# Second recurrence's input stage, tile by tile: three key tiles summed beside the first low-rank product

## The chip, the core and the metric

The kernel runs on one core of one Trainium2 chip. The metric is the device time of one execution in microseconds (us), the median of several runs. The engines are TensorE (PE, whose weight loads are listed apart as PEld), VectorE (DVE), ScalarE (ACT), GpSimd (POOL) and SyncE (SP, which issues the weight transfers).

## What is computed

The whole program is a two-layer hybrid network followed by a second two-layer network with a large expert lookup, in float32, for 272 tokens (256 and 16 learned ones) of width 1024. The change touches one piece of it, the inputs of the second layer's recurrence:

```python
def rwkv7_time_mix(h, mu, w_r, w_k, w_v, w0, w1, w2, a0, a1, a2, g1, g2, k_k, k_a, r_k, ln_w, ln_b, w_o):
    xx = jnp.pad(h, ((0, 0), (1, 0), (0, 0)))[:, :L] - h
    xr, xw, xk, xv, xa, xg = [h + xx * mu[i] for i in range(6)]
    r = xr @ w_r
    k = xk @ w_k
    v = xv @ w_v
    w_log = -jax.nn.softplus(-(w0 + jnp.tanh(xw @ w1) @ w2)) - 0.5
    a = jax.nn.sigmoid(a0 + (xa @ a1) @ a2)
    g = jax.nn.sigmoid(xg @ g1) @ g2
    kk = l2_normalize((k * k_k).reshape(B_, L, H, N))
    k = k * (1 + (a - 1) * k_a)
    ...
```

`h` is the normalized state. `w1` and `a1` are 1024 x 64, `g1` is 1024 x 160, the key, value and receptance weights are 1024 x 1024.

## The kernel before

The state lies with features on the 128 partitions: eight tiles (`KD` = 8) of 128 features by 272 tokens. Each engine has its own instruction list, written out by hand and run in that order; semaphores (`wait_ge`, `then_inc`) are the only order between engines. A `phase` is one block of such lists, with a barrier behind it. The function `rwkv` has the phase that this change edits, then the recurrence.

In that phase DVE finishes the norm (`norm_dve`, L244), writes eight tiles of `xn` (L1595), the difference to the previous token `xx` in two instructions over all tiles (L1598, L1599), and then blends `xn + mu * xx` with eight instructions per input (`blend`, L1553): first the one for the decay product, into `mix_a`, then the one for the rate product, into `mix_b`. Semaphores `mixed_w`, `mixed_a`, `mixed_k`, `mixed_g` count the finished tiles of each.

PE runs, in this order: the decay input product `w1` and the rate input product `a1` (both L1503, eight matmuls each with 64 output columns); their two output products (L1510, 8 + 8 matmuls, each waiting for a free bank among four "side" banks, 4 to 7); the eight key tiles (`project`, L1486, banks 0 to 3 in turn); the two gate input products (L1519); eight pairs of gate output products (L1524, L1525), which first wait for ACT's two gate sigmoids; the value tiles with the head sums (L1486, L1534); the receptance tiles. Every float32 matmul appears in the trace as two passes, so "x16" is eight matmuls.

ACT takes the side banks: Tanh and Copy (L1647) into `hw`, sixteen sigmoids (L1651) into `cum` and `a_`. Then for each key tile `m` it waits for `cum_ready` and, from `m` = 2, for DVE's key tile `m` - 2 (`grown_read`), and runs three exponentials (L1656 to L1658). Behind the last come `decay_mid` and `decay_end` (L1659, L1660) and only then the gate sigmoids (L1664).

DVE, when the decay values are there, sums them up in two halves (`sum_decay`, L1562 to L1567), blends the gate input, and takes each key tile with six instructions (`take_key`, L1574 to L1581), the first three of which read the bank and the last three of which need ACT's exponentials.

SP loads the key weights: the first four tiles in the phase before, the others when the first tiles are done (`k_ready`).

Of the kernel before, what the change touches and what calls it, by code (L numbers as in the profile page):

```python
# [12 lines left out]
ALU = mybir.AluOpType  # L13
# [278 lines left out]
def first_block(nc, a, w, x, xn, norm, late_const, cst, vcs, psum, psum_all):  # L292
# [1151 lines left out]
    def rwkv(g, kept, lora):  # L1444
# [3 lines left out]
        with ExitStack() as cx:  # L1448
# [3 lines left out]
            with ExitStack() as c0:  # L1452
                cum = sb("rw_cum", [P, KD, TP], c0)
                xx = sb("xx", [P, KD, T], c0)
                mix_a, mix_b = sb("mix_a", [P, KD, T], c0), sb("mix_b", [P, KD, T], c0)
                hw = bonus[0:64, 0:2, :]
                temp = norm.squares
                hg = temp[:, 0, :], temp[0:32, 1, :]
# [3 lines left out]
                with phase(nc, *NORM, "mixed_w", "mixed_a", "mixed_k", "mixed_g", "mixed_v", "mixed_r", "side", "side_read", "k_ready", "k_free",  # L1462
# [9 lines left out]
                    def _(pe):  # L1472
# [27 lines left out]
                        for n, (wt, src, mixed) in enumerate(((lora.w1, mix_a, S.mixed_w), (lora.a1, mix_b, S.mixed_a))):  # L1500
                            for q in range(KD):
                                pe.wait_ge(mixed, q + 1)
                                mm = pe.matmul(side_bank(n)[0:64, :], wt[:, q, :], src[:, q, :], start=(q == 0), stop=(q == KD - 1))  # L1503
                            mm.then_inc(S.side, 1)
# [6 lines left out]
                        for m in range(KD):  # L1511
                            if m >= 4:
                                pe.wait_ge(S.k_free, m - 3)
                            project(0, m, mix_a, S.mixed_k, S.k_ready)
                        for n, (m0, mn) in enumerate(((0, P), (P, 32))):
# [4 lines left out]
                            mm.then_inc(S.side, 1)  # L1520
                        pe.wait_ge(S.side_read, GATE_OUT)
# [24 lines left out]
                    def _(dve):  # L1546
# [23 lines left out]
                        def take_key(m):  # L1570
# [5 lines left out]
                            dve.scalar_tensor_tensor(out=k[:, m, 0:T], in0=temp[:, m % 2, :], scalar=1.0, in1=banks[m % 4], op0=ALU.add, op1=ALU.mult).then_inc(S.k_free, 1)  # L1576
                            dve.wait_ge(S.exps, m + 1)
# [16 lines left out]
                        for m in range(KD):  # L1594
                            last = dve.scalar_tensor_tensor(out=xn[:, m, :], in0=x[:, m, :], scalar=gain[:, m:m + 1], in1=norm.rs[:, :],  # L1595
                                                            op0=ALU.mult, op1=ALU.mult)
                        step(last)
                        dve.tensor_scalar(xx[:, :, 0:1], xn[:, :, 0:1], -1.0, None, ALU.mult)  # L1598
                        step(dve.tensor_tensor(xx[:, :, 1:T], xn[:, :, 0:T - 1], xn[:, :, 1:T], ALU.subtract))  # L1599
                        blend(MU_W, mix_a, S.mixed_w)  # L1600
                        blend(MU_A, mix_b, S.mixed_a)
# [4 lines left out]
                        blend(MU_K, mix_a, S.mixed_k)  # L1606
                        sum_decay(slice(0, 4))
                        sum_decay(slice(4, 8))
                        dve.wait_ge(S.side, 2)
                        blend(MU_G, mix_b, S.mixed_g)  # L1610
                        dve.wait_ge(S.k_ready, 1)
                        step(dve.memset(k[:, :, T:TP], 0.0))
                        for m in range(KD):
                            take_key(m)
                        dve.wait_ge(S.k_ready, KD)
# [26 lines left out]
                    def _(act):  # L1642
# [18 lines left out]
                        act.wait_ge(S.k_free, KD)  # L1661
# [7 lines left out]
                        def square_key(m):  # L1669

                            if m >= 2:
                                act.wait_ge(S.side, KK_SUM + m - 1)
                            act.wait_ge(S.kk_raw, m + 1)
                            act.activation(temp[:, m % 2, :], kk[:, m, 0:T], ACT.Square).then_inc(S.kk_squares, 1)

                        square_key(0)
# [1611 lines left out]
```

## Time and profile before

| What | Value |
|---|---|
| Median of 3 runs | 3508.43 us (3508.38 to 3513.5) |
| The profiled execution's own time | 3508.08 us |
| Its span in the trace | 3506.3 us |
| Mean granted TensorE clock | 0.957 of full |
| PE busy | 91% of the span |
| DVE busy | 63% of the span |
| ACT busy | 20% of the span |

The span is what the profiler records of the core; 1.8 us of that execution lie around it. The phase of the change runs from about 963 to 1109 us of the span. In rows of the timeline, the first number is the start, the second the time to the end of the last of the merged instructions, and the bracket the idle time ahead of them and who ended it. Clock 1.00 is 2.4 GHz, 0.50 is 1.2 GHz.

### The profile page before, as it was taken

The numbers are of one execution on the slowest core, as the hardware profiler recorded it, in microseconds if no ns is written. First come the engines' busy times: TensorE is split into PE (matmuls) and PEld (weight loads), VectorE is DVE, ScalarE is ACT, GpSimd is POOL, SyncE is SP. The second block draws the span as 40 slices with busy tenths as digits, with TensorE's granted clock in tenths as the row PEclk, the third lists the DMA queues.
The fourth block names the chain that finished last, engine by engine and source line by source line (L and its number), as shares of the span: only waits on it lengthen the run. The fifth ranks groups of instructions, "written<-read, shape, count | busy, mean of one in ns | idle before, by whom it ended". The sixth has DMA issues, their size and how long they took to land. (4 is left out here: it accounts for less than half of the span.)

```text
span 3506.3 us, 54158 instructions
## 1 busy us (share of the span) xinstructions
PE 3179.8 (91%) x20154; PEld 2378.5 (68%) x20154; DVE 2199.1 (63%) x5583; ACT 710.7 (20%) x1749; POOL 595.9 (17%) x516
## 2 busy tenths in 40 slices
PE   8999889999989999999998978887899988888887
PEld 8997479999968979987885433343578864344433
DVE  7843648778676548732447777776414468677775
ACT  1110321111131211101322222222212322222222
POOL 0000000000000000000004544444100035444442
PEclk9999599999999999999998999999999999999988
DMA  5443014454412014452349999999634479999997
GB/s 188 161 167 121 1 61 157 161 180 173 141 58 88 4 73 169 161 203 84 120 192 389 421 421 422 422 421 422 274 128 157 168 289 421 421 422 422 422 422 329
DMA packets 116002, 829.00 MB, mean 236 GB/s; under 512 B 12784, under 2 KB 14320, under 8 KB 17424
## 3 DMA queue, kind: packets, MB, share of 16 engines
q0 software_dynamic: 73728, 536.90, 36.8%
q1 hardware_dynamic: 39488, 273.59, 21.4%
q10 hardware_dynamic: 2576, 15.59, 1.3%
q8 instruction: 146, 2.39, 0.3%
q14 instruction: 64, 0.52, 0.0%
HBM read 824.99 MB, written 1.05 MB: 236 GB/s over the span
## 5 line engine op out<-in xcount | busy, mean ns | idle before, releaser
L3013 PE MATMUL psum_all<-expert_rows,const_sb 128*128 128x512 f32 x2048 | 963.7, 628 | 186.1 <-ACT const_sb L2925 185.0
L2612 POOL DMA_INDIRECT expert_rows<-in_peer_uv_dram,head_experts x512 | 595.7, 1164 | 2865.6 <-issue 1944.4
L3013 PEld LDWEIGHTS psum_all<-expert_rows,const_sb 128*128 128x128 f32 x2048 | 401.4, 200 | 730.7 <-issue 468.7
L2764 DVE CUSTOM_DVE_ANT_0 expert_rows<-expert_rows,xn 128x1024 f32<-128x1024 f32 x512 | 616.7, 1223 | 263.2 <-DMA expert_rows<-in_peer_uv_dram,head_experts 259.2
L2268 PE MATMUL psum_all<-x,weight_ring 128*128 128x256 f32 x1024 | 228.6, 381 | 0.0
L2925 ACT ACTIVATE const_sb<-cst,head_weights 128x128 f32<-128x128 f32 x496 | 158.6, 390 | 324.4 <-DVE head_weights L2775 299.9
L2268 PEld LDWEIGHTS psum_all<-x,weight_ring 128*128 128x128 f32 x1024 | 191.7, 190 | 28.8 <-issue 3.5
L407 PE MATMUL psum_all<-xn,weight_ring 128*128 128x136 f32 (+1 forms) x1408 | 193.5, 281 | 15.4 <-PEq L174 9.5
L407 PEld LDWEIGHTS psum_all<-xn,weight_ring 128*128 128x128 f32 x1408 | 177.9, 193 | 16.2 <-DMA weight_ring<-in_ffn_in_dram 9.5
L280 PE MATMUL psum_all<-xn,weight_ring 128*128 128x272 f32 (+1 forms) x640 | 147.7, 394 | 2.5 <-DVE expert_rows L2211 1.4
L407 PE MATMUL psum_all<-xn,weight_sums 128*128 128x136 f32 (+1 forms) x1056 | 143.5, 279 | 0.6 <-DVEq L631 0.6
L280 PEld LDWEIGHTS psum_all<-xn,weight_ring 128*128 128x128 f32 x640 | 123.4, 193 | 26.4 <-DVE expert_rows L2211 2.2
L2921 ACT ACTIVATE dots<-dots 128x4 f32<-128x4 f32 x124 | 25.4, 205 | 560.5 <-DVE dots L2764 560.5
L407 PE MATMUL psum_all<-input_sums,weight_sums 128*128 128x136 f32 (+1 forms) x1056 | 133.2, 279 | 0.1
L407 PEld LDWEIGHTS psum_all<-xn,weight_sums 128*128 128x128 f32 x1056 | 131.8, 192 | 1.0 <-issue 1.0
L407 PEld LDWEIGHTS psum_all<-input_sums,weight_sums 128*128 128x128 f32 x1056 | 127.2, 192 | 0.4 <-issue 0.4
L516 ACT ACTIVATE gate<-gate 128x272 f32<-128x272 f32 (+1 forms) x88 | 37.5, 427 | 359.4 <-DVE gate L601 359.4
L561 DVE TENSOR_TENSOR weight_sums<-weight_ring 128x512 f32<-128x512 f32 (+1 forms) x102 | 68.4, 671 | 59.1 <-PE psum_all L407 55.7
L407 PE MATMUL psum_all<-hidden,weight_ring 128*128 128x136 f32 (+1 forms) x704 | 88.6, 278 | 0.0
L2995 PE MATMUL psum_all<-x,weight_ring 128*128 128x256 f32 x384 | 84.8, 379 | 0.0
L407 PEld LDWEIGHTS psum_all<-hidden,weight_ring 128*128 128x128 f32 x704 | 84.5, 190 | 0.0
L2995 PEld LDWEIGHTS psum_all<-x,weight_ring 128*128 128x128 f32 x384 | 73.0, 190 | 15.0 <-issue 5.7
(579 smaller groups left out, 4806.8 us busy)
## 6 DMA issues: line engine op xcount, KB each, us to landing
weight_ring<-in_ffn_in_dram SPq DMA_DIRECT2D x88, 1024.0 KB, 4.9
weight_ring<-in_w_in_dram SPq DMA_DIRECT2D x48, 1024.0 KB, 4.8
weight_ring<-in_ffn_out_dram SPq DMA_DIRECT2D x32, 1024.0 KB, 5.1
weight_ring<-in_ffn_out_dram SPq DMA_DIRECT2D x16, 768.0 KB, 4.3
weight_ring<-in_hyb_in_dram SPq DMA_DIRECT2D x12, 1024.0 KB, 4.9
weight_ring<-in_peer_q_dram SPq DMA_DIRECT2D x12, 1024.0 KB
expert_rows<-in_w_v_dram ACTq DMA_DIRECT2D x8, 1024.0 KB
weight_ring<-in_br_attn_dram SPq DMA_DIRECT2D x8, 1024.0 KB, 7.2
```

Source lines behind the costliest of these rows:

```text
L280: mm = pe.matmul(banks[s * halves + h], wt[:, h, k, :], rhs[:, k, :], start=(k == 0), stop=(k == ktiles - 1))
L407: mm = pe.matmul(out, left(j), right(j), start=first and j == js[0], stop=end and j == js[-1], skip_group_check=onto)
L516: act.activation(gate[:, p % 2, :], gate[:, p % 2, :], ACT.Silu).then_inc(S.gate_ready, 1)
L561: dve.tensor_tensor(ws[:, 0], wt[:, 1, :, 0, :], wt[:, 1, :, 1, :], ALU.add).then_inc(S.weight_sums, 1)
L2268: mm = pe.matmul(late_bank(t)[:, half * T2:(half + 1) * T2], wt[:, half, k, :], h[:, k, :], start=(k == 0), stop=(k == KD - 1))
L2612: pool.indirect_dma_start(out=rows[:, j, :], out_offset=None, in_=a["peer_uv"], in_offset=bass.IndirectOffsetOnAxis(ap=idx[:, n, j:j + 1], ...
L2764: dve.tensor_tensor_reduce(row, row, xt[:, n, :], 1.0, 0.0, ALU.mult, ALU.add, dots[:, n, j:j + 1]).then_inc(S.dotted, 1)
L2921: act.activation(dots[:, n, at], dots[:, n, at], ACT.Gelu_apprx_tanh).then_inc(S.gelus, 1)
L2925: act.activation(diag[:, j, :], ident, ACT.Copy, scale=wts[:, n, j:j + 1]).then_inc(S.diagonals, 1)
L2995: mm = pe.matmul(query_bank[:, c, :], wt[:, c, k, :], h[:, k, :], start=(k == 0), stop=(k == KD - 1))
L3013: mm = pe.matmul(sums(n, half), diag[:, j, :], rows[:, j, D + half * 512:D + (half + 1) * 512], start=False, stop=last and j == TOPK - 1)
```

## The change

It adds a third buffer `mix_c`, rewrites DVE's first steps tile by tile, and reorders all three engines' lists. `take_key` is cut in two: what reads the bank stays, what needs the exponentials becomes `grow_key`.

```diff
-                mix_a, mix_b = sb("mix_a", [P, KD, T], c0), sb("mix_b", [P, KD, T], c0)
+                mix_a, mix_b, mix_c = (sb(name, [P, KD, T], c0) for name in ("mix_a", "mix_b", "mix_c"))
-                hg = temp[:, 0, :], temp[0:32, 1, :]
+                hg = mix_c[:, 0, :], mix_c[0:32, 1, :]
...
# PE
-                        for n, (wt, src, mixed) in enumerate(((lora.w1, mix_a, S.mixed_w), (lora.a1, mix_b, S.mixed_a))):
-                            for q in range(KD):
-                                pe.wait_ge(mixed, q + 1)
-                                mm = pe.matmul(side_bank(n)[0:64, :], wt[:, q, :], src[:, q, :], start=(q == 0), stop=(q == KD - 1))
-                            mm.then_inc(S.side, 1)
+                        early_tiles = []
+                        for s in range(2):
+                            pe.wait_ge(w.landed[g % 2][s], 16)
+                            wt = w.slot(g % 2, s, W2).rearrange("p (h k m) -> p h k m", h=2, k=KD)
+                            early_tiles += [wt[:, 0], wt[:, 1]]
+                        for q in range(KD):
+                            pe.wait_ge(S.mixed_k, q + 1)
+                            for m in range(3):
+                                mm = pe.matmul(banks[m], early_tiles[m][:, q, :], mix_a[:, q, :], start=(q == 0), stop=(q == KD - 1))
+                                if q == KD - 1:
+                                    mm.then_inc(S.k_ready, 1)
+                            pe.wait_ge(S.mixed_w, q + 1)
+                            mm = pe.matmul(side_bank(0)[0:64, :], lora.w1[:, q, :], mix_b[:, q, :], start=(q == 0), stop=(q == KD - 1))
+                        mm.then_inc(S.side, 1)
+                        project(0, 3, mix_a, S.mixed_k, S.k_ready)
+                        for q in range(KD):
+                            pe.wait_ge(S.mixed_a, q + 1)
+                            mm = pe.matmul(side_bank(1)[0:64, :], lora.a1[:, q, :], mix_c[:, q, :], start=(q == 0), stop=(q == KD - 1))
+                        mm.then_inc(S.side, 1)
...
-                        for m in range(KD):
-                            if m >= 4:
-                                pe.wait_ge(S.k_free, m - 3)
-                            project(0, m, mix_a, S.mixed_k, S.k_ready)
...
+                        for m in range(4, KD):
+                            pe.wait_ge(S.k_free, m - 3)
+                            project(0, m, mix_a, S.mixed_k, S.k_ready)
...
# DVE
+                        for m in range(KD + 2):
+                            if m < KD:
+                                dve.scalar_tensor_tensor(out=xn[:, m, :], in0=x[:, m, :], scalar=gain[:, m:m + 1], in1=norm.rs[:, :],
+                                                         op0=ALU.mult, op1=ALU.mult).then_inc(S.xn_ready, 1)
+                            if 1 <= m <= KD:
+                                q = m - 1
+                                dve.wait_ge(S.xn_ready, q + 1)
+                                dve.tensor_scalar(xx[:, q, 0:1], xn[:, q, 0:1], -1.0, None, ALU.mult)
+                                dve.tensor_tensor(xx[:, q, 1:T], xn[:, q, 0:T - 1], xn[:, q, 1:T], ALU.subtract).then_inc(S.xx_ready, 1)
+                            if m >= 2:
+                                q = m - 2
+                                dve.wait_ge(S.xx_ready, q + 1)
+                                for mu, dst, mixed in ((mu_k, mix_a, S.mixed_k), (mu_w, mix_b, S.mixed_w)):
+                                    dve.scalar_tensor_tensor(out=dst[:, q, :], in0=xx[:, q, :], scalar=mu[:, q:q + 1], in1=xn[:, q, :],
+                                                             op0=ALU.mult, op1=ALU.add).then_inc(mixed, 1)
+                        blend(MU_A, mix_c, S.mixed_a)
...
                         dve.wait_ge(S.side, 1)
-                        blend(MU_K, mix_a, S.mixed_k)
+                        blend(MU_G, mix_b, S.mixed_g)
                         sum_decay(slice(0, 4))
+                        dve.wait_ge(S.side, GATE_IN)
+                        step(dve.memset(k[:, :, T:TP], 0.0))
+                        for m in range(4):
+                            take_key(m)
+                        grow_key(0)
+                        grow_key(1)
                         sum_decay(slice(4, 8))
-                        dve.wait_ge(S.side, 2)
-                        blend(MU_G, mix_b, S.mixed_g)
-                        dve.wait_ge(S.k_ready, 1)
-                        step(dve.memset(k[:, :, T:TP], 0.0))
-                        for m in range(KD):
+                        grow_key(2)
+                        grow_key(3)
+                        for m in range(4, KD):
                             take_key(m)
+                            grow_key(m)
...
# ACT
-                        act.wait_ge(S.k_free, KD)
                         for n in range(2):
                             act.wait_ge(S.side, GATE_IN + n + 1)
                             act.activation(hg[n], side_bank(GATE_IN + n)[0:hg[n].shape[0], :], ACT.Sigmoid).then_inc(S.side_read, 1)
...
+                        act.wait_ge(S.k_free, KD)
                         square_key(0)
```

On PE, from the end of the norm to the gate output products, the list before reads (`rw_v` holds `w1`, `rw_k` holds `a1` and `w2a2`, `rw_gate` holds `g1`, `weight_ring` the key weights; here "x8" counts matmuls, not passes):

```order
L231 MATMUL psum_all<-norm_sums,cst 128x272
L232 MATMUL psum_all<-norm_squares,cst 128x272
L1503 MATMUL psum_all<-mix_a,rw_v 64x272 x8
L1503 MATMUL psum_all<-mix_b,rw_k 64x272 x8
L1510 MATMUL psum_all<-rw_bonus,rw_k 128x272 x16
L1486 MATMUL psum_all<-mix_a,weight_ring 128x272 x64
L1519 MATMUL psum_all<-mix_b,rw_gate 128x272 x8
L1519 MATMUL psum_all<-mix_b,rw_gate 32x272 x8
L1524 MATMUL psum_all<-norm_squares,rw_v 128x272
```

With the change, the same place from the last of eight rounds (each an L1508 row and an L1512 row) on:

```order
L1508 MATMUL psum_all<-mix_a,weight_ring 128x272 x3
L1512 MATMUL psum_all<-mix_b,rw_v 64x272
L1486 MATMUL psum_all<-mix_a,weight_ring 128x272 x8
L1517 MATMUL psum_all<-mix_c,rw_k 64x272 x8
L1524 MATMUL psum_all<-rw_bonus,rw_k 128x272 x16
L1529 MATMUL psum_all<-mix_b,rw_gate 128x272 x8
L1529 MATMUL psum_all<-mix_b,rw_gate 32x272 x8
L1486 MATMUL psum_all<-mix_a,weight_ring 128x272 x32
L1537 MATMUL psum_all<-mix_c,rw_v 128x272
```

Three and then one key tile moved ahead of the rate product, the gate inputs moved ahead of the other four, and the decay product is spread over the first rounds: the number of output columns goes from 128 to 64 and back in each round.

On DVE, at the start of the phase, the list before reads:

```order
L244 RECIPROCAL norm_rs<-norm_rs 128x272
L1595 SCALAR_TENSOR_TENSOR xn<-x,vcs,norm_rs 128x272 x8
L1598 TENSOR_SCALAR xx<-xn 128x8
L1599 TENSOR_TENSOR xx<-xn 128x8x271
L1553 SCALAR_TENSOR_TENSOR mix_a<-xx,vcs,xn 128x272 x8
L1553 SCALAR_TENSOR_TENSOR mix_b<-xx,vcs,xn 128x272 x8
```

and with the change, up to the second tile's first instruction after the first two blends:

```order
L244 RECIPROCAL norm_rs<-norm_rs 128x272
L1613 SCALAR_TENSOR_TENSOR xn<-x,vcs,norm_rs 128x272 x2
L1618 TENSOR_SCALAR xx<-xn 128x1
L1619 TENSOR_TENSOR xx<-xn 128x271
L1613 SCALAR_TENSOR_TENSOR xn<-x,vcs,norm_rs 128x272
L1618 TENSOR_SCALAR xx<-xn 128x1
L1619 TENSOR_TENSOR xx<-xn 128x271
L1624 SCALAR_TENSOR_TENSOR mix_a<-xx,vcs,xn 128x272
L1624 SCALAR_TENSOR_TENSOR mix_b<-xx,vcs,xn 128x272
```

The first blend, which PE waits for, stood behind ten instructions of all tiles and now stands behind seven of single tiles.

Further down DVE's list, between the first half's decay sums and the fifth key tile, the changed order is this (L1597 is the last instruction of `grow_key(1)`; L1575 to L1580 are the second half's `sum_decay`; L1587 is the first of `take_key(4)`):

```order
L1597 TENSOR_TENSOR rw_k<-rw_k,norm_rs 128x272
L1575 SCALAR_TENSOR_TENSOR rw_kk_r<-early_cst,rw_cum 128x320 x4
L1577 COPY rw_decay_mid<-rw_kk_r 128x20
L1578 TENSOR_TENSOR rw_kk_r<-rw_kk_r,rw_decay_mid 128x1280
L1579 COPY rw_decay_end<-rw_kk_r 128x20
L1580 TENSOR_TENSOR rw_cum<-rw_kk_r,rw_cum 128x1280
L1594 TENSOR_TENSOR rw_a<-rw_a,norm_sums 128x272
L1596 TENSOR_SCALAR rw_bonus<-rw_k,vcs 128x272
L1597 TENSOR_TENSOR rw_k<-rw_k,norm_sums 128x272
```

Before, both `sum_decay` halves stood ahead of the first key tile; now the second half stands behind four `take_key` and two `grow_key`, and six key tiles' `grow_key` stand behind it. ACT's order is unchanged but for the wait on `k_free`.

## Rows read from the trace of the kernel before

**Rows 1.** The page's head

```profile
span 3506.3 us, 54158 instructions
```

**Rows 2.** Busy by stretch: length, PE, PEld, DVE, ACT, POOL, granted clock, DMA

```profile
974.21:1029.94 55.73, 55.00 (x224) 40.19 (x224) 48.26 (x109) 21.82 (x49) 0.00 (x0) 0.95 0.20 76
```

**Rows 3.** Timeline, from the key weights' load to the second low-rank product

```profile
942.64 0.80 SPq L196 DMA_DIRECT2D weight_ring<-in_rwkv_k_dram  x2
...
967.61 3.39 DVE L1595 SCALAR_TENSOR_TENSOR xn<-x,vcs,norm_rs 128x272 f32<-128x272 f32 x8
...
971.12 2.40 DVE L1599 TENSOR_TENSOR xx<-xn 128x2168 f32<-128x2168 f32 x1
973.56 3.39 DVE L1553 SCALAR_TENSOR_TENSOR mix_a<-xx,vcs,xn 128x272 f32<-128x272 f32 x8
...
974.21 6.56 PE L1503 MATMUL psum_all<-mix_a,rw_v 128*64 128x272 f32 x16 [8.95 <-DVE mix_a L1553]
...
980.61 3.83 PE L1503 MATMUL psum_all<-mix_b,rw_k 128*64 128x272 f32 x16
```

**Rows 4.** Stretches with their granted clock (columns as in rows 2)

```profile
974.21:979.75 5.54, 5.54 (x13) 2.86 (x14) 5.54 (x14) 0.00 (x0) 0.00 (x0) 0.50 0.01 3
...
1109.21:1112.75 3.54, 3.54 (x37) 3.54 (x39) 0.19 (x1) 0.00 (x0) 0.00 (x0) 0.53 0.01 2
...
1107.14:1109.21 2.07, 0.00 (x1) 0.03 (x1) 1.40 (x3) 0.00 (x0) 0.00 (x0) 1.00 0.00 0
...
516.00:524.00 8.00, 5.47 (x32) 4.44 (x31) 3.98 (x8) 1.62 (x5) 0.00 (x0) 1.00 0.26 79
```

**Rows 5.** Timeline, output products, sigmoids and decay sums

```profile
984.37 2.10 PE L1510 MATMUL psum_all<-rw_bonus,rw_k 64*128 64x272 f32 x8
984.48 0.39 ACT L1647 ACTIVATE rw_bonus<-psum_all 64x272 f32<-64x272 f32 x1 [3.28 <-PE psum_all L1503]
...
986.18 3.16 ACT L1651 ACTIVATE rw_cum<-psum_all,vcs 128x272 f32<-128x272 f32 x8
986.70 2.97 DVE L1562 TENSOR_TENSOR_SCAN rw_kk_r<-early_cst,rw_cum 128x320 f32<-128x320 f32 x4 [1.80 <-ACT rw_cum L1651]
...
993.17 2.97 DVE L1562 TENSOR_TENSOR_SCAN rw_kk_r<-early_cst,rw_cum 128x320 f32<-128x320 f32 x4
```

**Rows 6.** Timeline, key tiles on PE, DVE and ACT

```profile
992.42 29.60 PE L1486 MATMUL psum_all<-mix_a,weight_ring 128*128 128x272 f32 x128
...
1003.07 0.38 DVE L1612 MEMSET rw_k<- 128x384 f32 x1
1003.49 0.50 DVE L1574 TENSOR_SCALAR rw_kk_r<-psum_all,vcs 128x272 f32<-128x272 f32 x1
...
1004.64 0.43 DVE L1578 TENSOR_TENSOR rw_a<-rw_a,norm_sums 128x272 f32<-128x272 f32 x1
...
1005.74 0.50 DVE L1574 TENSOR_SCALAR rw_kk_r<-psum_all,vcs 128x272 f32<-128x272 f32 x1
1005.92 0.43 ACT L1656 ACTIVATE norm_sums<-rw_kk_r 128x272 f32<-128x272 f32 x1 [9.28 <-DVE rw_k L1581]
...
1017.19 0.43 ACT L1656 ACTIVATE norm_rs<-rw_kk_r 128x272 f32<-128x272 f32 x1 [1.04 <-DVE rw_k L1581]
...
1018.30 0.22 ACT L1659 ACTIVATE rw_decay_mid<-rw_decay_mid 128x40 f32<-128x40 f32 x1
```

**Rows 7.** Timeline, gate inputs, gate sigmoids, first gate outputs

```profile
1021.86 7.61 PE L1519 MATMUL psum_all<-mix_b,rw_gate 128*128 128x272 f32 x32
...
1025.61 3.35 PEld L1519 LDWEIGHTS psum_all<-mix_b,rw_gate 128*32 128x32 f32 x16 [0.36 <-issue]
1025.77 1.28 ACT L1664 ACT_TABLE_LOAD   x1 [7.12 <-PE psum_all L1519]
...
1029.94 0.73 PE L1524 MATMUL psum_all<-norm_squares,rw_v 128*128 128x272 f32 x2 [0.48 <-ACT norm_squares L1664]
...
1030.60 0.72 PE L1525 MATMUL psum_all<-norm_squares,rw_v 32*128 32x272 f32 x2
```

More of the change, by code:

```diff
@@ L1461, in rwkv @@
                 side_bank = lambda n: banks[4 + n % 4]
-                with phase(nc, *NORM, "mixed_w", "mixed_a", "mixed_k", "mixed_g", "mixed_v", "mixed_r", "side", "side_read", "k_ready", "k_free",
+                with phase(nc, *NORM, "xn_ready", "xx_ready", "mixed_w", "mixed_a", "mixed_k", "mixed_g", "mixed_v", "mixed_r", "side", "side_read", "k_ready", "k_free",
                            "v_ready", "v_free", "r_ready", "r_free", "cum_ready", "exps", "grown_read", "kk_raw", "kk_squares", "kk_root", "kk_done",
@@ L1576, in take_key, with grow_key @@
                             dve.scalar_tensor_tensor(out=k[:, m, 0:T], in0=temp[:, m % 2, :], scalar=1.0, in1=banks[m % 4], op0=ALU.add, op1=ALU.mult).then_inc(S.k_free, 1)
+                        def grow_key(m):
                             dve.wait_ge(S.exps, m + 1)
@@ L1593, in _ @@
                         gain = vec(vcs, "mix_norm", KD, KD)
-                        for m in range(KD):
[L1595 to L1601, printed above, removed]
+                        mu_k, mu_w = vec(vcs, "mu", MU_K * KD, KD), vec(vcs, "mu", MU_W * KD, KD)
+                        for m in range(KD + 2):
[14 more added lines that the diff above has]
+                        blend(MU_A, mix_c, S.mixed_a)
                         for t in (a_, kk, cum):
@@ L1605, in _ @@
                         dve.wait_ge(S.side, 1)
-                        blend(MU_K, mix_a, S.mixed_k)
+                        blend(MU_G, mix_b, S.mixed_g)
                         sum_decay(slice(0, 4))
-                        sum_decay(slice(4, 8))
-                        dve.wait_ge(S.side, 2)
-                        blend(MU_G, mix_b, S.mixed_g)
-                        dve.wait_ge(S.k_ready, 1)
-                        step(dve.memset(k[:, :, T:TP], 0.0))
-                        for m in range(KD):
+                        dve.wait_ge(S.side, GATE_IN)
[4 more added lines that the diff above has]
+                        grow_key(1)
+                        sum_decay(slice(4, 8))
+                        grow_key(2)
+                        grow_key(3)
+                        for m in range(4, KD):
                             take_key(m)
+                            grow_key(m)
                         dve.wait_ge(S.k_ready, KD)
```

## The prediction, written before the changed kernel ran

> **What bounds the kernel now.** I read the head of the page first: the span is 3506.3 us [rows 1], and the profiled execution took 3508.08 us, 0.35 us under the median of 3508.43. The sum below is in the trace's time; what it saves or costs is taken off or put on the median. Next I read the stretches. From PE's first product of this phase to its first gate output product it is busy 55.00 of 55.73 us [rows 2], so in that stretch the phase is as long as PE's list, and a change can gain only by starting PE earlier, by cheaper PE work, or by removing the 0.73 us of waits. The timeline then shows what precedes the stretch: PE idles 8.95 us until the first blend of `mix_a` exists, while DVE does eight `xn` tiles (from 967.61), the two `xx` instructions (from 971.12), and starts blending at 973.56; PE starts at 974.21 [rows 3]. That head is what the change attacks. All else in the phase, from the gate outputs at 1029.94 on, is untouched in order, so I only have to ask: **when does the first gate output start now?** Its start at 1029.94 [rows 7] is my yardstick.
>
> **PE's earlier start.** A blend or `xn` tile costs 3.39/8 = 0.42 us [rows 3]. The `xx` instruction takes 2.40 us for 8 x 271 elements; a tile of it is then 0.30 plus a fixed part, and with the one-column instruction I take 0.44 per tile. Ahead of the first blend stand three `xn` and two `xx` tiles: 3 x 0.42 + 2 x 0.44 = 2.15, so it starts at 967.61 + 2.15 = 969.76 instead of 973.56, and with the same 0.65 us from there to PE, PE starts at 970.41: **3.80 us earlier**. From then on DVE needs 0.42 + 0.44 + 2 x 0.42 = 1.71 us per tile. A round on PE is eight passes, 8 x 0.229 = 1.84 us at clock 1.00 (a pass is (992.42 to 1021.86)/128 = 0.230 or, from the rate product, 3.67/16 = 0.229 [rows 3, 6, 7]) and 3.6 at 0.50, so PE is the slower and DVE stays ahead of it; as the first rounds run at 0.50, DVE would have to need over 2.2 us per tile to hold it up. The key weights were asked for at 942.64, 28 us ahead of PE's new start, so they are no new wait [rows 3].
>
> **The clock at the start.** PE ran at 0.50 for its first 5.54 us of work [rows 4], and the decay product took 6.40 us instead of 3.67. I take the same 5.54 us again. The nearest other restart kept 0.50 for 3.54 us [rows 4]; that would save half the difference, 1.0 us.
>
> **The rounds.** 64 passes: 5.54 us at 0.453 (6.40 us held 12 such and 4 fast ones) is 12 passes, the other 52 take 11.93, together 17.47 us. New is the change of shape, 128 to 64 columns and back, 16 times. No row has exactly that. Bounds: from the 128-column to the 32-column gate input, where the weight load starts 0.36 us late, 32 passes of 0.229 and the 0.16 us by which a row outlasts its passes (3.83 against 3.67) would end at 1021.86 + 7.34 + 0.16 = 1029.36, and the row ends at 1029.47 [rows 3, 7]: 0.1 per change. The gate outputs change from 128 to 32 rows at each matmul: 1029.94 to 1030.60 is 0.66 us for two passes instead of 0.46, so 0.2 per change [rows 7]. The lower end is 0: the loads may be hidden under the other passes. A column change is nearest to the first row, so I take 0.1: 1.6 us (ends: 0 and 3.2). The Trainium skill, "TensorE: Matmul & The Clock Gate", Part 2, step LDWEIGHTS, says that weight loads are pulled ahead of running matmuls where row groups don't conflict, or into the background buffer. By that the rounds would cost nothing extra; the gate output row, with its 0.2, shows that it is not so for every mix of shapes, and no row here shows it for this one.
>
> **From there to the gate outputs.** Rounds end at 970.41 + 17.47 + 1.6 = 989.5. Key tile 3 takes 3.67 (993.2), the rate product 3.67 and about 0.2 for its two shape changes (997.0). In the kernel before that point was 984.37 [rows 5]: the rate product, and with it ACT's and DVE's chain, is now **12.6 us later**, while PE's remaining work is shorter. So two chains meet at the gate outputs:
> - PE: output products 984.37 to 992.42 = 8.05, gate inputs 7.6, four key tiles 4 x 3.68 = 14.7: 30.4 us [rows 5 to 7], ready at 1027.4.
> - DVE and ACT. ACT releases the gate outputs behind the exponentials of key tile 7, which wait for `grow_key(5)`. From the start of the output products to the end of the first decay half: 993.17 - 984.37 = 8.80 [rows 5]. Memset 0.42. Four `take_key` of 1004.64 - 1003.49 = 1.15: 4.60. Two `grow_key` of 1005.74 - 1004.64 = 1.10: 2.20. Second decay half 993.17 - 986.70 = 6.47. Two `grow_key` 2.20, then keys 4 and 5 complete, 2 x 2.25 = 4.50 [rows 5, 6]. DVE sum: 29.19. Then ACT: 0.18 to start, 1017.19 to 1018.30 = 1.11 for the three exponentials, 0.35 for the two small ones, 1.29 table load, two sigmoids 0.7, 0.04 to PE: 3.67 [rows 6, 7]. Together **32.86 us**, ready at 1029.9.
>
> So the gate outputs start at 1029.9 against 1029.94. The head start of 3.8 us, and the wait of 0.48 that goes, are paid away: 1.8 us to changes of shape and 2.5 us to a new stall, PE waiting from 1027.4 to 1029.9 for the gate sigmoids, because DVE's decay sums now start late. Gain: **about 0.1 us**. DVE is done with key 7 some 3 us behind the old time, but the value blend (3.4 us) is needed only 10.5 us after the gate outputs begin, so nothing further is late.
>
> **A rule on the table load.** The switch from copy to sigmoid on ACT goes from 984.48 + 0.39 to 986.18: 1.3 us in all [rows 5], and that is what stands in my sum. The Trainium skill, "ScalarE: Activation LUTs", What ACT_TABLE_LOAD costs, puts a switch at about 2.66 us, since a drain of 1.38 comes with it. By that the new stall would be 1.4 us longer and the kernel 1.3 us slower. The row speaks against it.
>
> **The rivals.**
> 1. *Shape changes are free.* All chains shift by 1.8: gate outputs at 1028.1, gain 1.9, 3506.5 us. For: another weight load can hide; against: rows 7.
> 2. *They cost 0.2 each.* 1.6 us later: 3509.9.
> 3. *The new stall lowers the clock.* Ahead of the recurrence PE idled 2.07 us and then ran 3.54 us at 0.50; inside 516 to 524 it idled 2.5 us and the clock stayed at 1.00 [rows 4]. So it can go either way. Price: 3.5 us at half rate, less what the gate outputs' shape gaps hide, 1.4 us: 3509.7. By the table-load rule the time would be about the same, 3509.7, by another cause.
> 4. *Slower, on one mechanism: the tile-by-tile rounds keep PE at 0.50.* If PE paused in each round for DVE, the clock might not rise until the rounds end. 52 passes at 0.453 instead of 0.229 are 11.6 us: 3519.9. It decides once over 31 passes more (7.1/0.224) run at 0.50. Against: DVE needs 1.71 us per tile, PE at 0.50 3.6, so no pause is left to it.
> 5. *DVE and ACT are not behind.* If the decay sums overlapped more than I think and the stall vanished, gate outputs start at 1027.4: gain 2.5, with free shapes 4.3, 3504.1. That is the most that this change can give; it is under 7 us.
>
> **How the numbers follow.** About 7 us, 0.2%, is what a measurement of this kernel can tell from no change. Chances: forecast (3508.3, own range 3507 to 3509.5) 0.35; rival 1 0.20; rival 2 0.12; rival 3 0.17 with the table-load rule's 0.03 in it; rival 4 0.02; rival 5 0.10; scatter or a shift elsewhere that leaves these cases 0.04. The costs' bounds give 3504.1 to about 3511.3 (rivals 2 and 3 together), and the shown runs spread by 5.1 us upward, so the range is 3504 to 3512.5. Only rival 4 and part of the scatter lie beyond 0.2% on the slow side, 0.03; on the fast side only scatter, 0.03; the rest, 0.94, is the same.
>
> **What the profile of the changed kernel would show.** PE's first L1508 pass 2.8 to 2.9 us behind the end of the norm's reciprocal; the L1512 passes on a grid of 1.84 us (free shapes) or 2.0 (0.1 each) at clock 1.00; rate product's end 12 to 13 us later than 984.37; a single wait of 2 to 3 us of PE ahead of L1537 with ACT's gate sigmoid as its releaser; the first L1537 within 2 us of 1029.9; the same durations from there on. The prediction would be wrong if PE waited inside the rounds for DVE, if the stall ahead of L1537 were over 4 us or absent, or if the clock stood at 0.50 beyond some 6 us.

## The result, and the profile after

The changed kernel takes 3515.05 us in the median of 20 executions (3507.85 to 3524.64), the kernel before 3507.77 us (3503.59 to 3513.85, 20 executions): a ratio of 1.0022 with a 95% interval of 1.0014 to 1.003. It is 7.3 us slower, outside my range of 3504 to 3512.5. The times fall into two kinds: ten of the 20 lie at 3507.9 to 3513.4 us, ten at 3516.7 to 3524.6 us. The median of 3515.05 lies between them, where no execution is: the middle of the first kind is 3511.8 us, 4.0 over the kernel before, that of the second 3521.4. The traced execution took 3508.97 us, so it is one of the first kind.

From the page of that execution, the head and PE's busy time; the span answers to [rows 1]:

```profile
span 3507.2 us, 54172 instructions
...
PE 3184.6 (91%) x20154; PEld 2378.6 (68%) x20154; DVE 2200.6 (63%) x5597; ACT 711.1 (20%) x1749; POOL 599.4 (17%) x516
```

The timeline of the phase's start, which answers to [rows 3], with one round of the later ones:

```profile
967.47 1.85 DVE L244 RECIPROCAL norm_rs<-norm_rs 128x272 f32<-128x272 f32 x1 [3.45 <-ACT norm_rs L238]
...
971.43 0.50 DVE L1624 SCALAR_TENSOR_TENSOR mix_a<-xx,vcs,xn 128x272 f32<-128x272 f32 x1
...
972.07 3.06 PE L1508 MATMUL psum_all<-mix_a,weight_ring 128*128 128x272 f32 x6 [5.06 <-DVE mix_a L1624]
...
975.06 1.17 PE L1512 MATMUL psum_all<-mix_b,rw_v 128*64 128x272 f32 x2
...
982.87 0.67 PE L1512 MATMUL psum_all<-mix_b,rw_v 128*64 128x272 f32 x2
...
983.48 1.64 PE L1508 MATMUL psum_all<-mix_a,weight_ring 128*128 128x272 f32 x6
985.05 0.67 PE L1512 MATMUL psum_all<-mix_b,rw_v 128*64 128x272 f32 x2
...
992.18 3.93 PE L1486 MATMUL psum_all<-mix_a,weight_ring 128*128 128x272 f32 x16
```

The trace starts 1.74 us later at this point than that of before, from stages that no edit touches, so I count from the start of the reciprocal. In the kernel before these rows, with the value tile behind the gate outputs, read:

```profile
965.73 1.85 DVE L244 RECIPROCAL norm_rs<-norm_rs 128x272 f32<-128x272 f32 x1 [3.45 <-ACT norm_rs L238]
...
1040.40 3.93 PE L1486 MATMUL psum_all<-mix_a,weight_ring 128*128 128x272 f32 x16
1044.17 0.62 PE L1534 MATMUL psum_all<-norm_squares,early_cst 128*128 128x272 f32 x2
```

PE starts after 4.60 us instead of 8.48: 3.88 us earlier. It never waits for DVE in the rounds, but a round takes 985.05 - 982.87 = 2.18 us (2.17 in the mean of five), against eight passes of 0.229 = 1.83.

The timeline from the output products to the value tiles answers to [rows 5 to 7]:

```profile
999.85 2.10 PE L1524 MATMUL psum_all<-rw_bonus,rw_k 64*128 64x272 f32 x8
...
1007.90 7.72 PE L1529 MATMUL psum_all<-mix_b,rw_gate 128*128 128x272 f32 x32
...
1015.54 14.93 PE L1486 MATMUL psum_all<-mix_a,weight_ring 128*128 128x272 f32 x64
...
1023.76 0.43 ACT L1686 ACTIVATE norm_sums<-rw_kk_r 128x272 f32<-128x272 f32 x1 [6.36 <-DVE rw_k L1597]
...
1030.84 1.28 ACT L1693 ACT_TABLE_LOAD   x1
...
1032.13 0.66 ACT L1693 ACTIVATE mix_c<-psum_all 128x272 f32<-128x272 f32 x2
...
1032.85 0.73 PE L1537 MATMUL psum_all<-mix_c,rw_v 128*128 128x272 f32 x2 [2.37 <-ACT mix_c L1693]
1033.51 0.72 PE L1538 MATMUL psum_all<-mix_c,rw_v 32*128 32x272 f32 x2
1034.16 0.72 PE L1537 MATMUL psum_all<-mix_c,rw_v 128*128 128x272 f32 x2
...
1043.30 3.93 PE L1486 MATMUL psum_all<-mix_a,weight_ring 128*128 128x272 f32 x16
```

PE waits 2.37 us for the gate sigmoids, as forecast, and the gate outputs begin 65.38 us after the reciprocal's start instead of 64.21. They take 1043.30 - 1032.85 = 10.45 us, the same as before (1029.94 to 1040.40). In this execution the gate outputs and all behind them come 1.2 us later, and nothing in it explains a median 7 us up. For that a trace of the second kind was needed.

### The profile page after: what moved, and what is told of

Its sections match the earlier page's. It is cut to its first block and busy times, and to the rows that moved or that the text cites. A ratio compares the mean times of both kernels' runs of the same rounds, so it can differ in the third digit from the quotient of the medians.

```text
span 3507.2 us, 54172 instructions
## 1 busy us (share of the span) xinstructions
PE 3184.6 (91%) x20154; PEld 2378.6 (68%) x20154; DVE 2200.6 (63%) x5597; ACT 711.1 (20%) x1749; POOL 599.4 (17%) x516
```

## The experiments

Three theories stood against each other for the second kind of execution. **A**: the rounds, with their changes of shape, hold PE at 0.50 for much longer. **B**: the new wait ahead of the gate outputs lets the clock fall, and the gate outputs then keep it at 0.50. **C**: the time is lost elsewhere. "Phase" below is the time from the start of the reciprocal to the first head-sum product of the value tiles, 78.44 us in the kernel before (1044.17 - 965.73; 78.53 in a second trace of it) and 79.60 in the first trace of the changed one. Every set of runs has executions of the kernel before beside it on the same chip, and the ratios are to those; their medians are 3508.33 us for `again1`, `four1`, `gate1` and `both1`, 3508.97 for `stall`, `dense`, `late` and `group`, and 3508.32 for `short`, `again_b`, `group_a` and `before_a`.

### The changed kernel again

Label `again1`, no edit.

> The changed kernel once more, unedited, for its spread and a second trace. All theories: a median 3 to 13 us over the kernel before, and times from about 3508 to 3525 us. If the trace falls on a slow execution it tells at once where the time is: theory A (the rounds of three key tiles and one decay product keep PE at 0.50 for much longer than 5.9 us) has the rounds at some 30 us instead of 20.1; theory B (PE's wait of 2.4 us ahead of the gate outputs lowers the clock) has the rounds at 20 us and the gate outputs at 14 to 17 us instead of 10.5; theory C (the time is lost elsewhere, in the expert stage or by where the code lies) has neither.

All five executions took 3517.37 to 3522.51 us, median 3520.01 (ratio 1.0036, 1.0023 to 1.005), and the trace, with a span of 3515.8 us, is one of the second kind. Its timeline of PE at the gate outputs:

```profile
1021.80 3.83 PE L1486 MATMUL psum_all<-mix_a,weight_ring 128*128 128x272 f32 x16
1027.99 1.28 PE L1537 MATMUL psum_all<-mix_c,rw_v 128*128 128x272 f32 x2 [2.36 <-ACT mix_c L1693]
1029.19 1.27 PE L1538 MATMUL psum_all<-mix_c,rw_v 32*128 32x272 f32 x2
1030.39 1.28 PE L1537 MATMUL psum_all<-mix_c,rw_v 128*128 128x272 f32 x2
...
1046.04 1.27 PE L1538 MATMUL psum_all<-mix_c,rw_v 32*128 32x272 f32 x2
1047.24 6.08 PE L1486 MATMUL psum_all<-mix_a,weight_ring 128*128 128x272 f32 x16
1053.16 0.62 PE L1547 MATMUL psum_all<-norm_squares,early_cst 128*128 128x272 f32 x2
```

and its stretches (length, busy of PE, PEld, DVE, ACT, POOL, granted clock, DMA):

```profile
1026.00:1028.50 2.50, 0.51 (x1) 0.50 (x2) 2.40 (x8) 1.92 (x3) 0.00 (x0) 0.85 0.01 3
1028.50:1050.00 21.50, 21.50 (x38) 9.67 (x37) 7.02 (x17) 3.50 (x9) 0.00 (x0) 0.50 0.00 1
1050.00:1054.00 4.00, 4.00 (x15) 3.14 (x15) 0.00 (x0) 0.58 (x2) 0.00 (x0) 0.80 0.00 0
```

The wait is the same 2.36 us, but behind it every two passes take 1.20 us instead of 0.66, at clock 0.50, to the end of the gate outputs and through most of the first value tile. Gate outputs: 1047.24 - 1027.99 = 19.25 us instead of 10.45; value tile 1053.16 - 1047.24 = 5.92 instead of 3.77. Together 10.95 us. The phase is 90.7 us; the rounds are as in the first trace, with the clock back at 1.00 some 6 us after PE's start. The clock had fallen at 1027.73, 2.1 us into the wait, and was back at 1051.62. This is theory B's picture and not A's. Outside the phase the two traces of this kernel differ too, by 5.0 us less ahead of the reciprocal and 2.5 us more behind the phase, so of the 11.1 us in the phase 8.6 are left in the span. Note that the profile shows PE 100% busy all through those 21.5 us.

A third set of the unedited kernel, `again_b`:

> The changed kernel a third time, on the same chip as the others of this call. Half or more of the executions at 3516 us and over, the rest at 3508 to 3513. In its trace the gate outputs take either 10.5 us at clock 1.00 or 17 to 19 us, mostly at 0.50; nothing between and no other place that differs by more than 3 us.

Six executions, median 3521.01 us (ratio 1.0035, 1.0023 to 1.0047): 3510.26 and 3512.17, and four from 3520.90 to 3524.36, with nothing between. The traced one is the 3510.26: the phase is 79.6 us, the wait 2.37 us, no fall. That no other place would differ by over 3 us failed: the reciprocal starts at 965.7 us here, at 962.5 in `again1`, at 967.5 in the first trace. Over the two sets 9 of 11 executions are of the second kind, in the first measurement 10 of 20.

### Rounds of one shape

Label `four1`.

```diff
-                            for m in range(3):
+                            for m in range(4):
                                 mm = pe.matmul(banks[m], early_tiles[m][:, q, :], mix_a[:, q, :], start=(q == 0), stop=(q == KD - 1))
...
+                        for q in range(KD):
                             pe.wait_ge(S.mixed_w, q + 1)
                             mm = pe.matmul(side_bank(0)[0:64, :], lora.w1[:, q, :], mix_b[:, q, :], start=(q == 0), stop=(q == KD - 1))
                         mm.then_inc(S.side, 1)
-                        project(0, 3, mix_a, S.mixed_k, S.k_ready)
```

> All four early key tiles in the rounds, so that a round is eight passes of one shape, and the decay product behind them in one piece; everything else as in the changed kernel. In the trace every theory expects a round at 1.84 us instead of 2.17, the rounds with the decay product and key tile 3 some 2.5 us shorter, the gate outputs 2.5 us earlier, the wait ahead of them still 2.4 us. Theory A expects the executions around 3520 to be gone: all times at 3504 to 3510 us, at or 1 to 2 us under the kernel before. Theory B expects them to stay, in about half of the executions, as the wait is still there: from 3505 up to 3522. Theory C expects both kinds too.

Median 3517.43 us over eight executions (3510.74 to 3518.82), ratio 1.0023 (1.0013 to 1.0034). Five of the eight are above 3516 us: the second kind stays, so theory A is out. In its trace PE waits 1028.00 to 1030.35, the clock falls at 1032.6, 2.3 us after the gate outputs began, and is back at 1.00 at 1053.1; its stretches, in the columns of `again1`:

```profile
1028.00:1032.60 4.60, 2.25 (x7) 1.18 (x8) 4.50 (x13) 2.68 (x7) 0.00 (x0) 1.00 0.01 2
1032.60:1053.10 20.50, 20.50 (x38) 10.14 (x38) 5.29 (x13) 3.10 (x8) 0.00 (x0) 0.50 0.00 1
```

The gate outputs start 2.6 us earlier than in the first trace, as expected, and the phase is 86.5 us. Gate outputs and first value tile take 23.8 us against 14.2 in the kernel before: the fall costs 9.5 us here.

### Gate sigmoids earlier

Label `gate1`.

```diff
                         for m in range(KD):
+                            if m == 4:
+                                for n in range(2):
+                                    act.wait_ge(S.side, GATE_IN + n + 1)
+                                    act.activation(hg[n], side_bank(GATE_IN + n)[0:hg[n].shape[0], :], ACT.Sigmoid).then_inc(S.side_read, 1)
                             act.wait_ge(S.cum_ready, m // 4 + 1)
...
-                        for n in range(2):
-                            act.wait_ge(S.side, GATE_IN + n + 1)
-                            act.activation(hg[n], side_bank(GATE_IN + n)[0:hg[n].shape[0], :], ACT.Sigmoid).then_inc(S.side_read, 1)
```

> The gate sigmoids of ScalarE moved ahead of the exponentials of key tile 4, where ScalarE otherwise waits 6 us for the second half of the decay sums; one more table load there, everything else as in the changed kernel. In the trace every theory expects PE's wait of 2.4 us ahead of the gate outputs to go, and the gate outputs 2.4 us earlier. Theory B expects the executions around 3520 to be gone: all times at 3504 to 3511 us. Theory A expects them to stay, each 2.4 us less: about 3506 to 3522. Theory C expects both kinds too.

Median 3509.67 us over 11 executions (3506.71 to 3515.69), ratio 1.0008 (0.9999 to 1.0017). No execution is at 3516 or above, where theory A and C wanted about half. Against the 3520.01 of `again1`, on the same chip, removing one wait of 2.4 us took 10 us off the median, and the wait alone can't do that. Theory B's upper end was missed: five of the 11 lie above 3511. In the trace the wait is gone, the clock stays at 1.00 from 976.8 to the end of the phase, and the phase is 77.2 us; that is the second fastest of the 11 executions, so it doesn't show what the slower ones do.

### Both

Label `both1`, the two edits together.

> Both edits together: rounds of one shape and early gate sigmoids. Gate outputs some 4 to 5 us earlier than in the changed kernel, counted from the end of the norm. Theories A and B both expect only the fast kind of execution, 3502 to 3508 us, some 3 to 4 us under the kernel before. Theory C still expects about half of the executions 10 us longer.

Median 3507.9 us over 11 executions (3502.46 to 3510.99), ratio 0.9998 (0.9989 to 1.0007). The local part came as expected; from the timeline:

```profile
969.56 17.89 PE L1508 MATMUL psum_all<-mix_a,weight_ring 128*128 128x272 f32 x64 [5.07 <-DVE mix_a L1624]
987.39 3.88 PE L1513 MATMUL psum_all<-mix_b,rw_v 128*64 128x272 f32 x16
...
1010.56 14.93 PE L1486 MATMUL psum_all<-mix_a,weight_ring 128*128 128x272 f32 x64
...
1012.42 1.28 ACT L1686 ACT_TABLE_LOAD   x1
1013.72 0.67 ACT L1686 ACTIVATE mix_c<-psum_all 128x272 f32<-128x272 f32 x2
...
1018.75 1.28 ACT L1690 ACT_TABLE_LOAD   x1 [4.37 <-DVE rw_k L1597]
...
1025.33 0.62 PE L1537 MATMUL psum_all<-mix_c,rw_v 128*128 128x272 f32 x2
1025.88 0.72 PE L1538 MATMUL psum_all<-mix_c,rw_v 32*128 32x272 f32 x2
```

The first 64 passes take 987.39 - 969.56 = 17.83 us with one shape, against 992.18 - 972.07 = 20.11 with two; PE goes from the keys to the gate outputs without a wait. The phase is 74.49 us, 4.0 less than before, yet the median is only 0.4 us under that of before, where 3 to 4 were expected, and five of the 11 lie above 3508. The traced execution is the fastest. More on this below.

### The wait alone, in the kernel before

The direct test of theory B: labels `stall` and `short` repeat the second gate sigmoid in the kernel before, each time waiting for its own end.

```diff
                         for n in range(2):
                             act.wait_ge(S.side, GATE_IN + n + 1)
+                            for _ in range(5 if n else 0):
+                                step(act.activation(hg[n], side_bank(GATE_IN + n)[0:hg[n].shape[0], :], ACT.Sigmoid))
```

> The kernel before, with the second gate sigmoid repeated five times, so that PE waits some 2.5 to 2.8 us ahead of the gate outputs instead of 0.48; nothing else changed. If a wait there costs only itself, all executions are 2.2 us longer, about 3510.5. Theory B (the wait lowers the clock, and the gate outputs that follow keep it at 0.50 until the value tiles) expects in addition some 10 us in half or more of the executions: times from 3508 to 3524, a median of 3515 to 3520. Theory A (the rounds) has no rounds here and expects 3510.5.

Median 3518.7 us over nine executions (3514.85 to 3520.4), ratio 1.0027 (1.0017 to 1.0037). A wait of 2.56 us in the place of 0.48 costs the kernel before 9.7 us, and not one of the nine is at the 3510.5 us of a wait that costs only itself. Its trace shows where, on PE's timeline:

```profile
1032.46 0.72 PE L1524 MATMUL psum_all<-norm_squares,rw_v 128*128 128x272 f32 x2 [2.56 <-ACT norm_squares L1666]
1033.12 0.72 PE L1525 MATMUL psum_all<-norm_squares,rw_v 32*128 32x272 f32 x2
...
1034.42 0.92 PE L1525 MATMUL psum_all<-norm_squares,rw_v 32*128 32x272 f32 x2
1035.27 1.27 PE L1524 MATMUL psum_all<-norm_squares,rw_v 128*128 128x272 f32 x2
1036.47 1.27 PE L1525 MATMUL psum_all<-norm_squares,rw_v 32*128 32x272 f32 x2
```

The first pair and a half run at full rate, then the clock falls, 2.4 us after PE has resumed, and stays at 0.50 for 20.5 us, until 1055.3. The phase is 90.15 us, 11.7 more than before: 2.1 are the longer wait and 9.5 the fall. With `range(2 if n else 0)`:

> The kernel before with the second gate sigmoid repeated twice instead of five times: PE waits about 1.4 us ahead of the gate outputs (0.48 before, 2.6 in the run with five). If a wait there costs in proportion, all times are 0.9 us longer, about 3510. If it works through the fall of the clock, the share of executions that fall shrinks with the wait: median 3510 to 3514 us, with a few times at 3518 and over.

Median 3512.48 us over 11 executions (3506.86 to 3515.95), ratio 1.0011 (1.0002 to 1.002). No execution reached 3516, and the traced one, with a wait of 1.31 us, has no fall; the phase is 79.4 us. But that is the fastest of the 11, so it doesn't show whether slower ones had a short fall. The few times at 3518 and over that were expected did not come. The median is 4.2 us up where the wait explains 0.8; where the other 3 us go in these executions is not shown.

### Gate outputs in groups

Label `dense`: the changed kernel with its wait, but denser gate outputs.

```diff
-                        for m in range(KD):
-                            side_free(GATE_OUT + m)
-                            pe.matmul(side_bank(GATE_OUT + m), lora.g2[:, m * P:(m + 1) * P], hg[0], start=True, stop=False)
-                            pe.matmul(side_bank(GATE_OUT + m), lora.g2b[:, m * P:(m + 1) * P], hg[1], start=False, stop=True).then_inc(S.side, 1)
+                        for first in (0, 4):
+                            for m in range(first, first + 4):
+                                side_free(GATE_OUT + m)
+                                pe.matmul(side_bank(GATE_OUT + m), lora.g2[:, m * P:(m + 1) * P], hg[0], start=True, stop=False)
+                            for m in range(first, first + 4):
+                                pe.matmul(side_bank(GATE_OUT + m), lora.g2b[:, m * P:(m + 1) * P], hg[1], start=False, stop=True).then_inc(S.side, 1)
```

> The changed kernel with the wait of 2.4 us kept, but the gate outputs in two groups of four: four 128-row matmuls, then four 32-row ones, so that the shape changes 4 times instead of 16. In a trace at clock 1.00 the gate outputs take 8.0 us instead of 10.5. If it is the pauses between shapes that keep the clock at 0.50 once it has fallen, a fall lasts 3 to 7 us here instead of 20 and costs 2 to 3 us: all times at 3505 to 3513 us. If the wait alone decides, and the pauses don't matter, slow executions stay at 3516 or more.

Median 3512.63 us over 11 executions (3509.64 to 3518.02), ratio 1.0012 (1.0003 to 1.0021): one execution above 3516, and five above the 3513 that were the expected end. The trace caught a fall, and shows how short it is:

```profile
1033.30 3.62 PE L1538 MATMUL psum_all<-mix_c,rw_v 128*128 128x272 f32 x8 [2.36 <-ACT mix_c L1695]
1036.85 2.10 PE L1540 MATMUL psum_all<-mix_c,rw_v 32*128 32x272 f32 x8
1038.88 2.10 PE L1538 MATMUL psum_all<-mix_c,rw_v 128*128 128x272 f32 x8
...
1042.93 3.94 PE L1486 MATMUL psum_all<-mix_a,weight_ring 128*128 128x272 f32 x16
```

The clock fell at 1033.0 and was back at 1.00 at 1036.4, 3.1 us after PE resumed. All eight pairs took 9.63 us in spite of it, and the phase is 78.9 us. In `again1` the clock fell at the same point of the same wait (2.1 us into it in both), so the two differ by the order of the gate outputs: 3.4 us at 0.50 here, 23.9 there. The alternation of shapes is what holds the clock down; that it works by the pauses at each change is the likely reason, not shown apart. It is one trace of a short fall, but the times bear it out: one of 11 executions above 3516, against 19 of 31 of the changed kernel. The median is still 3.7 us over the kernel before, of which the phase explains 0.4.

### The head start alone, undone

Label `late`: as `both1`, with VectorE's start as in the kernel before.

```diff
-                        for m in range(KD + 2):
...
+                        for m in range(KD):
+                            last = dve.scalar_tensor_tensor(out=xn[:, m, :], in0=x[:, m, :], scalar=gain[:, m:m + 1], in1=norm.rs[:, :],
+                                                            op0=ALU.mult, op1=ALU.mult)
+                        step(last)
+                        dve.tensor_scalar(xx[:, :, 0:1], xn[:, :, 0:1], -1.0, None, ALU.mult)
+                        step(dve.tensor_tensor(xx[:, :, 1:T], xn[:, :, 0:T - 1], xn[:, :, 1:T], ALU.subtract))
+                        blend(MU_K, mix_a, S.mixed_k)
+                        blend(MU_W, mix_b, S.mixed_w)
```

> As the kernel with one shape in the rounds and early gate sigmoids, but VectorE's old start: all xn tiles, both xx instructions over all tiles, then the key blend and the decay blend in one piece each. What the tile-by-tile start is worth by itself: PE's first product 3.4 to 3.8 us later, counted from the end of the norm, and the gate outputs as much later; 3.5 us slower than the kernel with both edits, 3509 to 3513 us.

Median 3509.82 us over 11 executions (3507.8 to 3515.3), ratio 1.0007 (0.9998 to 1.0016). PE's first product comes 8.49 us after the reciprocal's start against 4.60, 3.9 us later (3.8 in the prediction), but the phase is 78.04 us against 74.49: 3.55 us. PE's first work runs at 0.50 for 5.4 us here and for 6.0 in `both1`, and that takes back 0.3. In the medians, each set against its own runs of the kernel before, `late` is 0.9 us over and `both1` 0.4 under: the start is worth 1.3 us there, where 3.5 were expected.

### All three, and the kernel before again

Label `group`: both edits and the grouped gate outputs.

> Both edits (rounds of one shape, early gate sigmoids) and the gate outputs in groups of four. No wait over 0.5 us ahead of the gate outputs, and these 2.4 us shorter: in a trace the value tiles start 7 us earlier than in the kernel before, counted from the end of the norm. Theory B expects only fast executions, 3500 to 3508 us, a median some 4 us under the kernel before.

Median 3508.44 us over 11 executions, ratio 0.9995 (0.9986 to 1.0004). The gate outputs on PE's timeline:

```profile
1028.46 2.00 PE L1538 MATMUL psum_all<-mix_c,rw_v 128*128 128x272 f32 x8
1030.39 2.10 PE L1540 MATMUL psum_all<-mix_c,rw_v 32*128 32x272 f32 x8
1032.41 2.10 PE L1538 MATMUL psum_all<-mix_c,rw_v 128*128 128x272 f32 x8
1034.44 2.10 PE L1540 MATMUL psum_all<-mix_c,rw_v 32*128 32x272 f32 x8
1036.47 3.93 PE L1486 MATMUL psum_all<-mix_a,weight_ring 128*128 128x272 f32 x16
```

They take 8.01 us instead of 10.45, and the phase 72.1, 6.4 us less than before. The median is 0.5 us under the kernel before, where some 4 were expected. Once more, with a second trace (`group_a`), and the kernel before itself (`before_a`):

> The kernel with both edits and grouped gate outputs once more, for its time and a second trace. The phase at 72.0 us as in its first trace. If the 5 us that its first trace lost between the recurrence's end and the next network were chance, that stage is at 353 us now and the median comes to 3503 to 3505 us; if they belong to the kernel, it is at 357 again and the median at 3508.

> The kernel before once more, for a second trace of it: how far do stages that no edit touches differ between two executions of one kernel. Median at 3508 to 3509 us; the phase of the change at 78.5 us from the norm's reciprocal to the first head sum of the value tiles; the stage from the recurrence's end to the next network's first layer at 352 to 354 us, the rest within 3 us of the first trace.

`group_a`: median 3506.83 us over 11 executions (3503.37 to 3508.83), ratio 0.9994 (0.9985 to 1.0003). `before_a`: 3508.14 us, ratio 1.0001 (0.9992 to 1.001). The stage from the recurrence's end (the first product of its last norm) to the next network's first layer takes 357.4 and 357.1 us in the two traces of `group`, 352.6 and 353.0 in those of the kernel before. So 4.4 of the 6.4 us are given back there, both times: of the two cases that I had written down, chance is out. It isn't `group`'s code alone either: the trace of `short`, where nothing of that stage and nothing of DVE's order was edited, has 356.5. Around the recurrence's output norm the clock falls twice in every trace: for 6.8 us each in the kernel before, for 10.2 us each in `group`, for 6.8 and 10.2 in `short`. Other stages differ between two traces of one kernel: one ahead of the phase takes 185.7 and 182.2 us in the kernel before, over the 3 us that I expected as the most.

## Why the prediction was wrong

Point by point, by its own steps:

- **PE's earlier start**: 3.80 forecast, 3.88 measured. Right. DVE needs 1.65 us per tile (1.71 forecast), and PE never waits for it in the rounds.
- **The clock at the start**: 5.54 forecast, 5.7 us measured at 0.50 (972.07 to 977.80). Right.
- **The rounds**: 17.47 + 1.6 = 19.07 us forecast, 20.11 measured. The term of the shape changes was mis-sized: a round is 0.34 us longer than eight passes, 0.17 per change, where I took 0.1 within ends of 0 and 0.2. With the slightly longer low stretch that is 1.0 of the 1.2 us by which the first trace's gate outputs miss; the rest is in the chain below.
- **From there to the gate outputs**: DVE's and ACT's chain 32.86 us forecast, 1032.85 - 999.85 = 33.00 measured; the new wait 2.5 forecast, 2.37 measured. Right, to a tenth or two.
- **The table load**: 1030.84 to 1032.13, 1.29 us, and no drain behind it. By the Trainium skill's rule ("ScalarE: Activation LUTs", What ACT_TABLE_LOAD costs) it would be 2.66; this trace disagrees and the measurement decides.
- **The step that failed is the price of rival 3, "the new stall lowers the clock"**: "3.5 us at half rate, less what the gate outputs' shape gaps hide, 1.4 us". The sum itself, 3508.3 us, had this cost at nothing. The runs show 10.95 us in `again1` and 9.5 in `four1` and `stall`. It is what takes the median out of the range: the first kind's middle, 3511.8 us, is inside, the second's, 3521.4, is not. It is also the one of my signs of being wrong that came true, the clock at 0.50 beyond some 6 us. I took the length of the low stretch from dense work behind another gap [rows 4], and put it onto gate outputs that alternate between 128 and 32 rows. `again1`, `four1` and `stall` show that such work did not bring the clock back: it stayed at 0.50 for 20 to 24 us, into the first value tile. `dense` shows the cause: the same wait with grouped shapes has 3.4 us at 0.50, and its gate outputs are 1.6 us longer than the 8.01 of `group`, close to my 1.4. And I had counted the shape gaps as a relief, as time that the low clock doesn't lengthen; two passes took 1.20 us instead of 0.66, the gap lengthened with them.
- **The chance of that rival**, 0.17, was also low: 19 of 31 executions of the changed kernel are of the second kind. The rows I had seen (a fall behind a gap of 2.07 us, none behind one of 2.5 us) are two of eleven gaps of PE over 2 us in the first 1600 us of that trace. At two, of 2.52 and 2.43 us, the clock stayed at 1.00; one, of 8.95, lies in a low stretch already begun; at the other eight, of 2.07 to 5.71 us, it fell, in the gap or up to 2.4 us behind it. All of them had to be read before a new one of 2.5 could be priced.
- **"Slower, on one mechanism"**, rival 4, had a price (3519.9) near the second kind's times, but that is chance: its place, the rounds, has no waits and the clock was back after 5.7 us. The time went at the gate outputs.

What is shown: the wait costs about 10 us where the clock falls (`stall` in the kernel before; `gate1` without the wait; the traces of `again1`, `four1`, `stall`). Of the changed kernel itself one execution of the second kind was traced, and two of the first; that the others are like them rests on their times. What stays open: executions of the first kind are still some 4 us over the kernel before (3511.8 against 3507.8 in the middle), of which the phase explains 1.2; and `both1` and `group` gain 4.0 and 6.4 us in the phase, but 0.4 to 1.5 us in the median. It is a pattern: in `gate1`, `late`, `both1`, `dense`, `short` and `group` alike the median lies 1.3 to 5.8 us above what the phase of the trace would give. The stage behind the recurrence takes part of it in `group`; why it does was not tried. The traces of `both1`, `gate1` and `short` are of the fastest or second fastest execution of their sets, so they may not show the rest.

## What to carry to other kernels

A wait of two microseconds on PE is not priced by its length: look at what PE does behind it, since work that alternates between shapes ran at 1.2 GHz to its end after such a wait, in three traces of three kernels. Group matmuls of one shape (2.4 us saved in 10.5 in this phase, though the median of `group` did not show it), and place the one instruction that PE will wait for where its engine is idle anyway. When an early start on one engine is bought with a later chain on others, sum the chain to the point where they meet, and then ask what the new wait does to the clock.

## What was not expected of the hardware

A change between a 128-column and a 64-column weight tile costs PE 0.17 us in float32 with 272 columns moving (a round of 2.17 us with two changes, 1.83 without), between 128 and 32 rows 0.2 us at 2.4 GHz and 0.3 at 1.2 GHz (1.20 us for two passes of 0.453). The Trainium skill ("TensorE: Matmul & The Clock Gate", Part 2, step LDWEIGHTS) has weight loads pulled ahead of running matmuls; these runs show it for equal shapes only. In the rounds of `both1` each load starts 0.229 us, one pass, ahead of its matmul; in those of the changed kernel the first load of a new shape starts with its matmul, behind 0.36 or 0.41 us without a load.

The clock can fall after PE is back at work: 2.3 us after it in `four1`, 2.4 in `stall`. And a profile in which PE is 100% busy may hide a low clock: the busy time counts the gaps between shapes too, and only the granted clock, 0.50 for 21.5 us of 100% in `again1`, tells.

The falls keep to some places. Ahead of this phase PE idles 3.16 us in each of the 14 traces, and in all of them the clock falls 2.5 to 2.9 us after the start of that gap. Two traces of one kernel tend to repeat such places, as the 357.4 and 357.1 us of `group` do.
